# First FFN, up stage: two of its eight pairs of row blocks computed with seven block products instead of eight

## The reference, cut to what matters

```python
h = rmsnorm(x, norm_ffn[l])
x = x + (jax.nn.silu(h @ w_gate[l]) * (h @ w_up[l])) @ w_down[l]
```

## Time and profile before

| | us |
|---|---|
| median of 3 runs | 2469.32 |
| the profiled execution | 2469.4 |
| its span | 2467.7 |
| TensorE (PE) busy | 2461.9 (100%) |
| DVE busy | 1496.4 (61%) |
| ACT busy | 1207.9 (49%) |
| POOL busy | 626.7 (25%) |
| DMA queue of SP, share of the 16 engines | 73.2% |

### The profile page before, as it was taken

How to read it: one execution, slowest core, us unless ns; L and a number is a source line. 1 busy time by engine, 2 the same in 40 slices (tenths; PEclk the granted TensorE clock), 3 DMA queues, 4 the chain that set the end, 5 groups by cost and what they waited for, 6 DMA issues and landing times.

```text
span 2467.7 us, 30451 instructions
## 1 busy us (share of the span) xinstructions
PE 2461.9 (100%) x10976; PEld 2038.2 (83%) x10976; DVE 1496.4 (61%) x1723; ACT 1207.9 (49%) x1623; POOL 626.7 (25%) x537
## 2 busy tenths in 40 slices
PE   9999999999999999999999999999999999999999
PEld 7888888888888888888888888888888888888887
DVE  5766666555455555565455565576567647665665
ACT  6555445444344434455444544544555545553553
POOL 3665524210012100131011322332334103320330
PEclk9999999999999999999999999999999999999999
DMA  9888868776677667687667667777787767776775
GB/s 251 215 203 212 208 193 228 209 203 202 192 203 210 201 194 204 201 241 203 176 204 197 196 202 201 210 212 223 221 218 203 218 193 219 219 209 194 202 227 177
DMA packets 491587, 511.70 MB, mean 207 GB/s; under 512 B 187121, under 2 KB 290005, under 8 KB 491345
## 3 DMA queue, kind: packets, MB, share of 16 engines
q1 hardware_dynamic: 490112, 507.88, 73.2%
q0 software_dynamic: 1088, 2.07, 0.3%
q10 hardware_dynamic: 272, 0.26, 0.0%
HBM read 467.38 MB, written 2.11 MB: 190 GB/s over the span
## 4 chain that ended last, share of the span: by engine, by line
PE 53%; DMA 0%; DVE 0%; ACT 0%; POOL 0%; issue 0%
PE ps L617 17%; PE ps L619 17%; PE ps L618 17%; DMA raw<-in_w_in 0%; PE ps L954 0%; PE ps L715 0%; PE ps L700 0%; DVE w_lo L1417 0%; PE ps L934 0%; ACT w_hi L1021 0%; PE ps L889 0%; PE ps L888 0%; PE ps L725 0%; ACT z L1060 0%; POOL rstd L2151 0%
## 5 line engine op out<-in xcount | busy, mean ns | idle before, releaser
L1417 DVE TENSOR_TENSOR w_lo<-raw,w_hi 128x1024 fp32r<-128x1024 f32 x880 | 1152.2, 1312 | 924.2 <-ACT w_hi L1021 921.5
L1021 ACT ACTIVATE w_hi<-raw 128x1024 fp32r<-128x1024 f32 x879 | 929.4, 1059 | 1142.7 <-PE ps L619 1080.3
L617 PE MATMUL ps<-w_hi,xT_hi 128*128 128x512 f32 x2200 | 862.3, 392 | 0.3 <-ACT z L1060 0.2
L619 PE MATMUL ps<-w_hi,xT_lo 128*128 128x512 f32 x2200 | 856.7, 389 | 0.0
L618 PE MATMUL ps<-w_lo,xT_hi 128*128 128x512 f32 x2200 | 856.2, 389 | 0.0
L617 PE MATMUL ps<-w_hi,yT_hi 128*128 128x512 f32 x1312 | 511.4, 390 | 0.0
L619 PE MATMUL ps<-w_hi,yT_lo 128*128 128x512 f32 x1312 | 510.5, 389 | 0.0
L618 PE MATMUL ps<-w_lo,yT_hi 128*128 128x512 f32 x1312 | 510.5, 389 | 0.0
L617 PEld LDWEIGHTS ps<-w_hi,xT_hi 128*128 128x128 f32 x2200 | 413.0, 188 | 88.6 <-issue 2.5
L619 PEld LDWEIGHTS ps<-w_hi,xT_lo 128*128 128x128 f32 x2200 | 413.0, 188 | 86.0
L618 PEld LDWEIGHTS ps<-w_lo,xT_hi 128*128 128x128 f32 x2200 | 413.1, 188 | 85.2
(11 more groups left out here) (214 smaller groups left out, 923.2 us busy)
## 6 DMA issues: line engine op xcount, KB each, us to landing
raw<-in_w_up SPq DMA_DIRECT2D x264, 512.0 KB, 4.3
raw<-in_w_down SPq DMA_DIRECT2D x176, 512.0 KB, 4.6
raw<-in_w_in SPq DMA_DIRECT2D x160, 512.0 KB, 4.1
raw<-in_w_gate SPq DMA_DIRECT2D x88, 512.0 KB, 4.4
raw<-in_w_out SPq DMA_DIRECT2D x60, 512.0 KB, 4.7
raw<-in_w_in SPq DMA_DIRECT2D x128, 192.0 KB, 3.0
raw<-in_w_in SPq DMA_DIRECT2D x192, 128.0 KB, 2.8
raw<-in_w_proj_m SPq DMA_DIRECT2D x16, 512.0 KB, 4.3
```

What stands on the lines that cost most here:

```text
L617: pe.matmul(o, hi[:, q], w_hi[n % NS][:, k, 0:width], start=first, stop=False)
L619: mm = pe.matmul(o, lo[:, q], w_hi[n % NS][:, k, 0:width], start=False, stop=last)
L1021: nc.scalar.activation(w_hi[n % NS][:, :, 0:width], raw[n % NS][:, :, 0:width], ACT.Copy).then_inc(hi_ready, 1)
L1417: v.tensor_tensor(w_lo[n % NS][:, :, 0:width], raw[n % NS][:, :, 0:width], f32(w_hi[n % NS][:, :, 0:width]), ALU.subtract).then_inc(lo_rea ...
```

## The change

The 2048 rows make 8 pairs of row blocks. For pairs 0 and 1 the gate and the up product are computed together. With two token tiles, two row blocks and the two matrices (gate, up), a pair is a 2 x 2 by 2 x 2 product of blocks: 8 block products before, 7 after (a Strassen-like form), with sums of blocks as operands. Pairs 2 to 7 stay as they are.

A group now has 20 units instead of 16, in the order of the table `ORDER`; below they are called places 0 to 19. Places 0 and 1 are gate pairs 2 and 3 (12 matmuls each). Places 2 to 5 are pair 0: first, sums, crossed (6 matmuls each), last (3). Places 6 to 9 are pair 1, likewise. Places 10 to 13 are gate pairs 4 to 7, places 14 to 19 are up pairs 2 to 7 (12 each): 186 matmuls.

The pairs' raw blocks (1 MB for each pair, `pair_raw`) have their own buffers. POOL makes four sums of weight blocks for a pair (`terms`), ACT and DVE split them into slots of `w_hi` and `w_lo` in two instructions of 512 columns instead of one of 1024. Four shared sums gather in banks 4 to 7; DVE adds them to the gate and up results (`mix`, `gate_sum`, first half of `product`). POOL also makes the sums of activation blocks once (`sum_x`: four scalings and four sums of 256 columns), which ACT and DVE split into `xs_hi`, `xs_lo` at the end of the stage before. The loops over groups are written out, and some semaphores are merged.

```diff
+ORDER = [("gate", 2), ("gate", 3), *((part_, j_) for j_ in range(SUMMED_PAIRS) for part_ in PARTS),
+         *(("gate", u_) for u_ in range(4, 8)), *(("up", u_) for u_ in range(2, 8))]
...
-    asked = [*quarters("out_a", 4, False), *groups("ffn1", (15,)), *quarters("ffn1_down2", 6, True), *quarters("proj_a", 4, False),
+    asked = [*quarters("out_a", 4, False)[:2], GROUP_AT[0], GROUP_AT[0] + ORDER.index(("gate", 3)), *summed_groups(), *quarters("ffn1_down2", 6, True), *quarters("proj_a", 4, False),
...
+    def summed_groups():
+        return [GROUP_AT[k + 1] + 11 if k + 1 < GROUPS and FIRST_OF[k + 1] > 0 else GROUP_AT[k] + len(ORDER) - 1 + AHEAD for k in range(GROUPS)]
...
+            def load_pair(k, j):
+
+                if k == 0:
+                    sp.wait_ge(ha.y_lo, FREE + HEADS)
+                else:
+                    sp.wait_ge(lo_ready, NS + PART_AT[k - 1, j, "last"] + 1)
+                for e, w in enumerate((a["w_gate"][0], a["w_up"][0])):
+                    sp.dma_start(pair_raw[j][:, e, :, :], rows(w)[j][:, :, k * W:(k + 1) * W]).then_inc(pair_landed[j], 16)
...
+                    if kind == "first":
+                        if u == 0:
+                            pe.wait_ge(mixed_step, 5 * k)
...
+                        product(4, xT, of_x(2 * u, 0), n, 0, done_)
+                        mm = product(7, xs, of_sums(u, 2), n, 1, done_)
+                    elif kind == "sums":
+                        product(5, xs, of_sums(u, 0), n, 0, done_)
+                        mm = product(6, xs, of_sums(u, 1), n, 1, done_)
+                    elif kind == "crossed":
+                        product(0, xT, of_x(2 * u + 1, 0), n, 0)
+                        mm = product(1, xT, of_x(2 * u + 1, 1), n, 1)
+                    elif kind == "last":
...
+                        mm = product(2, xs, of_sums(u, 3), n, 0)
...
+                if part == "first":
+                    act.wait_ge(pair_landed[j], 32 * (k + 1))
+                    nc.scalar.activation(hi[:, 0, :], gate_[:, 0, :], ACT.Copy)
+                    act.wait_ge(terms_ready, 4 * m + 1)
+                    nc.scalar.activation(hi[:, 1, :], term_up, ACT.Copy).then_inc(hi_ready, 1)
...
+                dve.wait_ge(hi_ready, n + 1)
+                for c, src in enumerate(srcs):
+                    op = v.tensor_tensor(w_lo[n % NS][:, c, :], src, f32(w_hi[n % NS][:, c, :]), ALU.subtract)
+                op.then_inc(lo_ready, 1)
...
+                    def mix(k):
+
+                        dve.wait_ge(mixed_step, 5 * k + 1)
...
+                        v.tensor_tensor(up_sum[:, 1, :], tok_gate[:, 0, :], ps[6][:], ALU.add).then_inc(mixed_step, 1)
+                        dve.wait_ge(mixed_step, 5 * k + 2)
+                        v.tensor_tensor(up_sum[:, 0, :], up_sum[:, 1, :], ps[5][:], ALU.add).then_inc(mixed_step, 1)
+                        v.tensor_tensor(tok_gate[:, 1, :], up_sum[:, 1, :], ps[7][:], ALU.add).then_inc(mixed_step, 1)
+                        dve.wait_ge(mixed_step, 5 * k + 4)
+                        v.tensor_tensor(up_sum[:, 1, :], tok_gate[:, 1, :], ps[5][:], ALU.add).then_inc(mixed_step, 1)
...
-                            v.scalar_tensor_tensor(tok_act[:, tt, :], tok_gate[:, tt, :], half_r_sq[:, tt:tt + 1], pair[1][tt][:],
-                                                   ALU.mult, ALU.mult).then_inc(by_dve, 1)
+                            v.tensor_tensor(up_sum[:, tt, :], up_sum[:, tt, :], pair[1][tt][:], ALU.add).then_inc(by_dve, 1)
+                        dve.wait_ge(tok_made, 4 * k + 2)
+                        for tt in range(NT):
+                            dve.wait_ge(by_dve, FREE + PH[up][BY_DVE] + 4 * i + 3 + tt)
+                            v.scalar_tensor_tensor(tok_act[:, tt, :], tok_gate[:, tt, :], half_r_sq[:, tt:tt + 1], up_sum[:, tt, :],
+                                                   ALU.mult, ALU.mult).then_inc(tok_made, 1)
...
+                            if u == 9 and i > 0:
                                 lo_part(fg0 - 1, i)
-                            own(u, i)
-                        turn(up, i, 16, behind)
+                            if u == 11:
+                                mix(k)
+                            if u == 14:
+                                gate_sum(k, i)
+                            if u == 16:
+                                gate(k, i)
+                            if u == 19:
+                                product(k, i)
+                        turn(up, i, len(ORDER), behind)
...
+            def terms(k, j):
...
+                def free(part):
+                    if before:
+                        pool.wait_ge(lo_ready, NS + PART_AT[(*before, part)] + 1)
...
+                free("first")
+                g_.tensor_tensor(term_up, up_[:, 1, :], up_[:, 0, :], ALU.subtract).then_inc(terms_ready, 1)
+                free("sums")
...
+                g_.tensor_tensor(term_first, up_[:, 0, :], gate_[:, 0, :], ALU.subtract).then_inc(terms_ready, 1)
+                pool.wait_ge(terms_ready, 4 * m + 1)
+                g_.tensor_tensor(term_second, term_up, gate_[:, 0, :], ALU.add).then_inc(terms_ready, 1)
+                free("crossed")
+                pool.wait_ge(terms_ready, 4 * m + 3)
+                g_.tensor_tensor(term_crossed, gate_[:, 1, :], term_second, ALU.subtract).then_inc(terms_ready, 1)
...
+            for k in range(1, GROUPS):
+                if FIRST_OF[k] == 0:
+                    turn_act(k - 1)
+                for j in range(SUMMED_PAIRS):
+                    terms(k, j)
+                if FIRST_OF[k] > 0:
+                    turn_act(k - 1)
```

324 lines of the change are left out of this document (226 added, 98 removed).

## The result

The changed kernel takes 2527.44 us (median of 4 runs, 2525.34 to 2528.48) against 2469.36 (4 runs): ratio 1.0234, 95% interval 1.0217 to 1.0252, 58 us slower. The forecast was 2485.5, the range ended at 2506. The profiled execution has a span of 2526.7 us, 59.0 more than before.

The account below looks back on a forecast made before the run. TensorE, busy 100%, was taken as the bound. Terms -15.0 + 4.4 + 17.6 + 2.1 + 5.6 + 1.5 = +16.2 on 2469.4 gave 2485.5 us; range 2464 to 2506, to hold 8 times in 10.

Parts of the forecast that it names:

- the 15.0 us: Up stage, 11 groups: 66 matmuls fewer at 0.2267 us each, 15.0 us less on TensorE.
- the place of the first gaps: Up stage after the change: TensorE idle in gaps before places 4, 6, 7 and 10.
- The start: Start of up stage: SP's load of place 1 waits for quarter 2 and transposes; 0 to 4 us, taken as +1.5.
- 0.4 us late in each of 11 groups: Place 10: load issued only once place 6 is split, block ready at 9.91 against 9.52; +4.4 us in all.
- place 12 "at nothing": Transposes and place 12's load behind them: lands at 13.0, split ends 15.4, no cover left; costed at nothing.
- The port term: Places 3 to 8: DVE and POOL take turns at the shared port, 2.2 us in each of 8 groups, +17.6 us.
- The burst: Four pair loads ahead of place 0's load make it 1.1 us late, pushing DVE toward place 4; 0.7 each, +5.6 us.
- The other 3 have no `product` and no halves there: Three groups without a former group of their part: only four sums against place 6's 0.74; 0.7 us each, +2.1.
- the forecast's own range: 2474 to 2500 us: port 1.0 to 3.9 in the 8 groups, burst 0 to 0.7, other terms as they stand.
- Rival B: Loads bound it: transfers take 0.25 us more each, transposes and bursts collide; +31.0, 2500.4 us; chance 0.20.
- Its sign: Mark of rival B in the profile: ACT waits for DMA at place 0 and the gaps sit at place 4.

Follow-up runs that it names:

- h_perm: f_late with the first group's pairs computed plainly, and there row blocks 0, 1 and 2, 3 changed round: 2468.71 us, ratio 0.9998.
- e_start: Changed kernel with sums of x behind quarter 1's halves, transposes of quarters 2 and 3 behind the loads of places 1 and 10: 2524.41 us, ratio 1.0221.
- f_sumx: e_early with the sums of x made by ACT and DVE instead of POOL: 2489.95 us, ratio 1.0083.
- g_plain: Changed kernel, first group computing its pairs plainly (192 matmuls, no sums of weights), sums of x made during it: 2516.08 us, ratio 1.0189.
- e_early: Changed kernel with loads of places 10 to 13 issued when their raw slot is free, transposes behind the load of place 13: 2495.01 us, ratio 1.0107.
- e_noterms: Changed kernel without POOL's sums of weights; ACT and DVE split raw blocks instead (other products): 2502.03 us, ratio 1.0133.
- h_dve: h_perm with spread pair loads, own buffers, and the sums of the 8 groups on DVE behind splits of places 19, 1, 2 and 4: 2471.06 us.
- f_late: e_early with POOL's halves of tok_act waiting for place 9's split, transposes and parts moved behind them: 2485.07 us, ratio 1.0063.
- k_pool: h_perm with product's second half behind place 12's split, transposes behind the load of place 16, parts behind place 19's split: 2464.74 us, ratio 0.998.
- k_dve: h_fin with transposes behind the load of place 16, parts behind place 19's split, DVE's first four sums behind places 16 and 17: 2459.55 us.
- e_own: Changed kernel with buffers of their own for pair 1's sums of weights: 2525.31 us, ratio 1.0226.
- f_v1: e_early plus f_sumx, f_late, reordered start DMAs, own buffers for both pairs, next group's pair loads behind loads of places 14 to 17: 2494.87 us.
- h_fin: h_dve with product's second half behind place 12's split and the sums earlier, behind places 17, 19, 1 and 2: 2483.41 us, ratio 1.0057.

## Why the prediction was wrong

The direction, the 15.0 us and the place of the first gaps were right. The sum failed in these steps.

- **"The start: ... 0 to 4 us, I take 1.5."** It cost 24.2, and this is the largest error. The step priced SP's wait for quarter 2 and not what stands ahead of quarter 1: 9.6 us of POOL's sums of x, 3.0 us of issuing pair loads ahead of the first unit's load, 5.98 us of transposes ahead of the second's. The earlier trace rows showed POOL's times in this place; from the earlier trace rows, 0.74 us for 256 columns, its eight new instructions could have been put at some 6 us of the 9.6. It did not price either that place 0 now needs quarter 1 of x (h_perm: 3.5 us of begin), nor that POOL's first sums lengthen DVE's work on the quarters of x, 5.74 instead of 1.67 in front of place 5. Taking these away one at a time gained 3 us in e_start, 5 in f_sumx and 11 in g_plain; how the 24.2 divide stays open.
- **"That is 0.4 us late in each of 11 groups", and place 12 "at nothing".** Place 10 was sized right (0.4 to 0.6 in the 8 groups). The same wait holds for places 11 to 13, each load tied to a split one place later, with the transposes in between: 19.1 us in the 8 groups instead of 3.2, and the larger part of the 5.6 in the two that open a part. e_early shows it, 32 us with what hung on it. The prediction had written that past place 12 no cover is left and each us costs a us; it then priced this at today's 3.2 and 4.4 us, and they became 4.8 and 5.
- **The port term, 17.6 at places 6 and 7.** It measured 15.8; the size was about right, by luck in parts. A sum takes 1.26 to 1.29 alone, as the slope of the earlier trace rows said, not the 1.04 of the earlier trace rows. The turns are real: e_noterms, without the sums, has 0.5 us of the 19.4. But they are one load among several on a stretch that is full. TensorE uses up places 2 to 9 in 9.5 us; DVE's 14 pieces of 0.6 are 8.4 and `product` 2.7. e_noterms shows that this much is still in time, h_dve that sums on DVE in the stretch cost as much as POOL's. Each thing taken out of it shortens the gaps: the halves (f_late, 10 us), half of `product` (k_pool against h_perm, from 7.9 to 3.4 us at places 4 to 7, with the transposes moved as well), at last the sums (k_dve, none). The shares in the changed kernel itself stay open.
- **The burst, 0.7 at place 4 in 8 groups, 5.6.** Place 4's gaps were 0.5 to 0.95 in 5 of the 8 groups, 3.6 in all, and the trace shows the step that was forecast. In these five ACT waits 3.6 to 4.4 us for the load of place 0 and starts on it 3.9 to 4.6 us before TensorE begins place 0; in the other three 6.5 to 7.8 before, and there is no gap. The worst but one, TensorE at place 0 at 829.09, and the same group of e_early, at 808.46:

```profile
825.05 1.06 ACT L1148 ACTIVATE w_hi<-raw 128x1024 fp32r<-128x1024 f32 x1 [4.29 <-DMA raw<-in_w_gate]
```
```profile
801.61 1.06 ACT L1151 ACTIVATE w_hi<-raw 128x1024 fp32r<-128x1024 f32 x1 [1.48 <-DMA raw<-in_w_gate]
```

But the burst alone does not do it: e_early keeps it, ACT starts on place 0 there 6.3 us or more before TensorE, and no gap is left. The lateness came with the late loads of the group before, which is argued from this comparison and not traced load by load.
- **"The other 3 have no `product` and no halves there", 0.7 us each.** The two groups that open a part lost nothing at places 4 to 7; their 5.6 us are 3.5 of gaps at places 10 and 11 and 2.1 of slower matmuls, most of these at the lower clock behind a pause of 1.9 us.
- Not in the sum at all: a gap costs more than its length. In the 8 groups the granted clock stays at 1.00, but the second matmul behind each pause comes 0.34 us after the first instead of 0.23; over some six pauses this is 0.8 us in a group.
- A slip without weight here: the forecast's own range begins at 2474, but its lowest terms (port 1.0 in 8 groups, burst 0) add up to 2470.4.

Rival B named loads without cover, which is right, and priced them from an extra 0.25 us for each load instead of following SP's queue. Its sign (ACT waits for the load of place 0, gaps at place 4) is there, but it is 3.6 us; most of the loss is at places 10 to 12.

The prediction leaned on the Trainium skill (SBUF — State Buffer, section Who interferes with whom). The runs here agree: a split of 1.23 becomes 2.31 and two gate products become 3.48 beside POOL's sums, and instructions of DVE with one operand in PSUM keep their 0.64 each beside them (784.04 in the group shown). The Trainium skill's page says that issue order decides who blocks; e_own shows what came of it for a queue that never paused: seven pieces of DVE went through at 0.6 each, and POOL's two halves took 7.16 us.

The Trainium skill's 2.5 cycles for an element (GPSIMD Engine Reference, section 2.1) gave an estimate of 1.07 us for a sum; the measured 1.26 to 1.29 decide.

## What to carry to other kernels

Saved work on the bounding engine shortens the time in which the others must deliver: write down, for the shortened stretch, each other engine's whole list of instructions against its length, and for each DMA the instruction that lets it go and all that is issued ahead of it. When a late thing is moved, look at once at what queues behind its new place: five of the runs here (e_own, e_start, f_v1, h_perm, h_fin) won a term and paid it again, whole or in part, at the next queue. The kernel came out faster than before only in k_pool and k_dve, when nearly all waits behind the first group were gone, and in k_dve DVE at 95% cost nothing.

## What the runs showed of the hardware

- After a stop of 12.6 us TensorE's matmuls came 0.43 us apart for 3 us, and again after 4.35 us of stop in the same group; 0.43 is nearly twice 0.2267, the lower of its two levels, 1.2 GHz instead of 2.4. The granted clock there, by window:

```profile
399.00:407.00 8.00, 2.18 (x5) 1.84 (x6) 5.33 (x9) 4.74 (x9) 1.35 (x1) 0.50 0.17 60
408.00:416.00 8.00, 7.98 (x35) 6.22 (x34) 5.41 (x6) 5.77 (x13) 8.00 (x7) 1.00 0.35 66
```

- Pauses of the same length did not always bring the clock down: f_v1 has five of 2.7 us at place 17, and behind three of them the granted clock fell to 0.5 and the matmuls lost 1.9 us in the group, behind the other two it stayed at 1.00 and they lost 0.3.
- Two transposes took SP 2.6 to 3.7 us to issue with at most one load issued in the 3 us before them, 4.0 to 4.9 behind two loads (the 8 groups of the changed kernel) and 5.98 at the start, and loads of 512 KB beside them landed after 5.3 us instead of 3.6.
